# A depthwise convolution's last chunks on one core: order of gates, taps and sums

## The chip, the cores and the metric

The program runs on one core of one Trainium2 chip. The metric is device time in microseconds (us). The median of three runs of the kernel before is 1395.32 us (1394.76 to 1398.21).

## The reference

A two-layer decoder step is computed in float32 for 512 prompt tokens and 32 sample tokens (8 sequences of 4), 1024 features. The change lies in the convolution module of layer 0:

```python
a = h @ w_pw1 + b_pw1
u = a[..., :D_MODEL] * jax.nn.sigmoid(a[..., D_MODEL:])      # the GLU
ext = jnp.concatenate([hist.astype(u.dtype), u], axis=1)
v = lax.conv_general_dilated(ext, w_dw[:, None, :], (1,), 'VALID', ...) + b_dw   # 31 taps, each feature alone
v = layernorm(v, g_ln, b_ln)                                 # mean and variance over the 1024 features
y = jax.nn.silu(v) @ w_pw2 + b_pw2
```

A squared-ReLU MLP, a shared latent K/V, attention, a second MLP and a last norm follow. They are untouched.

## The kernel before, in words

Features lie on the 128 partitions, so the 1024 features are 8 chunks (`DC`), and the 544 tokens lie along the free dimension. Chunks are numbered 0 to 7 here. What is called the fifth chunk in the diff's neighbourhood is chunk 4, the seventh is chunk 6, and the last is chunk 7.

Each engine has its own queue, written out by hand in one block of the program, and runs it strictly in that order. The engines meet at semaphores. For chunk c of the convolution the work is:

- TensorE: two matrix products, number 2c (the gate half) and 2c+1 (the other half), each of 48 matmuls of 128x272 (`product`, L1623). Two chunks later come `tap_products(c)` (L1661): the 31 taps cut into groups of 4, each tap a matmul of 32 columns of weights against 512 tokens, on four copies of the input that are shifted by 0 to 3 tokens (`shifted`). `pe_steps(c)` says how many groups of 4 TensorE takes: 6 (24 taps) for chunks 0 to 6, all 8 for chunk 7. The result goes to PSUM bank 4 or 5 in turn (`conv_bank`), and bank 0 for chunk 7. From chunk 2 on the tap products wait on `conv_used` for the bank that chunk c-2 used.
- VectorE: `gates(c)` (L1094) scales the gate half, `gated(c)` (L1101 to L1104) makes the GLU output and writes it to `ext`. `sample_taps(c)` (L1112, L1115) does the 31 taps of the 32 sample tokens. `psum_taps(k)` (L1135, L1136) adds the taps that TensorE left out, 7 of them, of the chunk three before (`LATER` = 3). `statistics(k)` (L1163, L1144, L1152) centres the chunk by an early mean, which lies in banks 6 and 7, and adds the chunk and its square to the running sums `acc` and `acc2`. Chunk 6 is done otherwise: `dve_taps(6)` (L1122, L1124) does its seven left-out taps from `ext` in SBUF, ahead of TensorE's, and `finish(6)` (L1128) adds the two parts. Once chunk 6 is in the sums VectorE signals `stat_in`. When chunk 7's taps are there (`conv_mm`), L1203 makes `v` of chunk 7.
- ScalarE: the high halves of weights (`high`, L703; `ahead(u)` does those whose place the product u frees), the sigmoid (L759), the squares (`squares_after`, L717), and for chunk 7 half of the DMA issues that make the shifted copies (L766). The other half, and all of them for the other chunks, are issued by SyncE's queue (`shift`, L513), with the tap weights (L514).
- GpSimd: the low halves of weights (`low`, L575), each after its high half.

After chunk 7's taps TensorE turns the sums over the features into the layernorm's mean and variance: `small_part` (L1711, matmuls with a single moving column, 5 for each sum) of `acc` and `acc2` once `stat_in` has come, `mean_part` (L1706) of `acc` into banks 6 and 7, then the same of chunk 7's `v` and of its square. VectorE computes the variance from L1216 on, ScalarE takes the root, TensorE spreads it (L1728), and the second pointwise product starts (`product_pair`, L1674).

The order of the work around the change on VectorE is this loop:

```python
for c in range(DC):
    k = c - LATER
    if k >= 0:
        psum_taps(k)
        ...
        statistics(k)
    gates(c)
    gated(c)
    sample_taps(c)
    if c == DC - 2:
        dve_taps(c)
psum_taps(DC - LATER)
statistics(DC - LATER)
```

Of the kernel before, what the change touches and what calls it, by code (L numbers as in the profile page):

```python
# [24 lines left out]
DC = D // P  # L25
# [4 lines left out]
HALF = T // 2  # L30
# [6 lines left out]
TAPS = 31  # L37
# [3 lines left out]
GROUPS = P // SB  # L41
PE_TAPS = 24
STEPS = (TAPS + GROUPS - 1) // GROUPS
# [3 lines left out]
LATER = 3  # L47
# [26 lines left out]
VEC, at = {}, 0  # L74
# [7 lines left out]
CON, at = {}, 0  # L82
# [105 lines left out]
def decoder_program(nc, xT, hist, vecs, diags, cons, rope_tab, rows0, page_table, cache_ckv, cache_kpe, w_pw1, w_pw2, w_up, w_down,  # L188
# [17 lines left out]
    with ExitStack() as ctx:  # L206
# [3 lines left out]
        def sem(name):  # L210
# [12 lines left out]
        acc = sb("acc", [P, T])  # L223
# [10 lines left out]
        acc2 = sb("acc2", [P, T], F32, tap_mem)  # L234
# [3 lines left out]
        ps = ctx.enter_context(nc.psum_tensor("ps", [P, 8, 512], F32))  # L238
# [22 lines left out]
        invd = sb("invd", [P, P], F32, conv_mem)  # L261
# [68 lines left out]
        stat_in, mean_mm, small_mm, var_out, rs_out, rs_mm = (  # L330
            sem(n) for n in ("stat_in", "mean_mm", "small_mm", "var_out", "rs_out", "rs_mm"))
# [80 lines left out]

        def pe_steps(c):

            return PE_TAPS // GROUPS if c < DC - 1 else STEPS

        def moved(c, s, g):
            n = NP + GROUPS * (pe_steps(c) - 1)
# [259 lines left out]
        def _(act):  # L678
# [53 lines left out]
            def squares_after(c):  # L732
                for k in STAT_AFTER.get(c, ()):
                    sq_in()
                    square(v[:, k, :])
# [16 lines left out]
            for c in range(DC):  # L752
                if c == 0:
                    ahead(1)
                else:
                    squares_after(c - LATER)
                    ahead(2 * c)
                gate_()
                af.activation(t1[:, :], t1[:, :], ACT.Sigmoid, bias=V("b_pw1", DC + c)).then_inc(gate, 1)  # L759
                if c == DC - 1:  # L760
                    act.wait_ge(u_out, 2 * c + 1)
                    act.wait_ge(conv_mm, c - SLOTS + 1)
                    for s in range(GROUPS):
                        for g in range(GROUPS // 2, GROUPS):
                            to, of = moved(c, s, g)
                            act.dma_start(to, of).then_inc(shift_in[c % SLOTS], 16)  # L766
                if c > 0:
                    ahead(2 * c + 1)
            squares_after(DC - LATER)
# [261 lines left out]
        def _(dve):  # L1031
# [60 lines left out]
            def gates(c):  # L1092
                dve.wait_ge(mm, 2 * c + 1)
                df.tensor_tensor(halves(t1[:, :]), acc_of(2 * c), halves(rstd[:, :]), ALU.mult).then_inc(gate_in, 1)  # L1094
                dve.wait_ge(gate_in, c + 1)
                dve.sem_inc(freed, 1)
# [19 lines left out]

            def dve_taps(c):
                dst = v[:, c, 0:NP]
                for k in range(PE_TAPS, TAPS):
                    w, a = V("w_dw", c * TAPS + k), ext[:, c, k:k + NP]  # L1120
                    if k == PE_TAPS:
                        link(df.tensor_scalar(dst, a, w, None, ALU.mult))  # L1122
                    else:
                        link(df.scalar_tensor_tensor(dst, a, w, dst, ALU.mult, ALU.add))  # L1124
# [51 lines left out]

            for c in range(DC):
                k = c - LATER
                if k >= 0:
                    psum_taps(k)  # L1180
                    if k == EARLY:
                        early_mean()
                    statistics(k)
                gates(c)
                gated(c)
                sample_taps(c)
                if c == DC - 2:
                    dve_taps(c)
# [4 lines left out]
            k = DC - 2  # L1193
# [360 lines left out]
            for i in range(NSC):  # L1554
                dve.wait_ge(ks_mm, i + 1)
                m = st[:, i % SETS, 0:1]
# [39 lines left out]
        def _(pe):  # L1596
# [48 lines left out]
            def run(u0, n, ah, al, fresh=True):  # L1645

                for j in range(n):
                    product(u0 + j, ah, al, fresh and j == 0)
                    if j == 0:
                        sums()  # L1650

            def tap_products(c):
                pe.wait_ge(shift_in[c % SLOTS], 16 * (GROUPS * GROUPS + 1) * (c // SLOTS + 1))
                if 2 <= c < DC - 1:
                    pe.wait_ge(conv_used, c - 1)
                if c == DC - 1:
                    pe.wait_ge(freed, 2 * DC)
                n = pe_steps(c)
                for k in range(n):
                    for g in range(GROUPS):  # L1660
                        m = tf.matmul(ps[SB * g:SB * (g + 1), conv_bank(c), 0:NP], diag[:, c % SLOTS, GROUPS * k + g, :],  # L1661
                                      shifted[:, c % SLOTS, g, GROUPS * k:GROUPS * k + NP], start=(k == 0), stop=(k == n - 1))
                m.then_inc(conv_mm, 1)
# [37 lines left out]
            tap_products(DC - 2)  # L1701
            tap_products(DC - 1)

            def mean_part(a, begin, end):
                for h in range(2):
                    m = tf.matmul(ps[:, 6 + h, 0:HALF], invd[:, :], a[:, h * HALF:(h + 1) * HALF], start=begin, stop=end)  # L1706
                return m

            def small_part(bank, at, a):
                for j, b in enumerate(blocks5):  # L1710
                    m = tf.matmul(ps[:, bank, at + 2 * j:at + 2 * j + 1], a[:, b], invd[:, 0:1], start=True, stop=True)  # L1711
                return m

            pe.wait_ge(stat_in, 1)
            small_part(5, 0, acc)
            small_part(5, 1, acc2).then_inc(small_mm, 1)
            mean_part(acc, True, False)
            pe.wait_ge(sq_src, DC)
            small_part(4, 0, v[:, DC - 1, :])
            pe.wait_ge(sq_out, 2 * DC)  # L1720
# [382 lines left out]
```

## Time and profile before

| what | us |
|---|---|
| median of 3 runs | 1395.32 |
| lowest, highest | 1394.76, 1398.21 |
| profiled execution, its own time | 1399.37 |
| its span | 1397.6 |
| TensorE busy | 1358.2 (97%) |
| VectorE busy | 811.8 (58%) |
| ScalarE busy | 601.3 (43%) |
| GpSimd busy | 726.3 (52%) |

The profile is of one execution. PE is TensorE's matmuls, PEld its weight loads, DVE VectorE, ACT ScalarE, POOL GpSimd, SP SyncE; a q behind the name means the engine's queue issuing a DMA. Times are microseconds from the span's start. An end of a matmul is modelled, so its duration overlaps the next one's start, and in these rows a float32 matmul counts as two (x48 is 24 matmuls) where it isn't of the type fp32r. The mean granted TensorE clock is 0.984 of full speed.

### The profile page before, as it was taken

What the parts mean: (1) busy time and instruction counts of PE and PEld (TensorE: products, weight loads), DVE (VectorE), ACT (ScalarE), POOL (GpSimd) and SP (SyncE); (2) the same over time, 40 slices, a digit from 0 to 9 for tenths busy, and PEclk for the clock granted to TensorE, in tenths of its full rate; (3) what the DMA queues carried; (4) which work ended last, traced back from release to release, by engine and by line L of the source; (5) the groups of instructions that cost most, each with busy time, mean ns of one, the idle gap of its engine ahead of it and who ended that gap; (6) DMA issues with size and microseconds to landing.
All of it is one profiled execution on the core that took longest, in us unless ns stands there. A gap on an engine that the chain in (4) does not pass through costs nothing.

```text
span 1397.6 us, 26262 instructions
## 1 busy us (share of the span) xinstructions
PE 1358.2 (97%) x11038; PEld 1264.9 (91%) x11038; DVE 811.8 (58%) x1224; ACT 601.3 (43%) x1016; POOL 726.3 (52%) x505
## 2 busy tenths in 40 slices
PE   6999889999999999999999999999999999999997
PEld 6877489999999999999899867678999999999997
DVE  6689557655545463766555656554676364545534
ACT  5211255443434443434666544442364444443432
POOL 3322153587888785333323444330437888787741
PEclk9999789999999999999999999999999999999998
DMA  5755302222233324322111577670223222222221
GB/s 210 197 163 146 109 31 91 91 91 91 92 102 103 98 91 157 117 91 66 35 35 53 181 294 263 265 264 2 91 85 97 91 91 91 91 91 92 95 86 64
DMA packets 107204, 160.66 MB, mean 115 GB/s; under 512 B 7568, under 2 KB 91792, under 8 KB 101840
## 3 DMA queue, kind: packets, MB, share of 16 engines
q1 hardware_dynamic: 99536, 116.50, 26.3%
q0 software_dynamic: 7168, 41.95, 8.0%
q8 instruction: 87, 1.43, 0.4%
q10 hardware_dynamic: 384, 0.55, 0.1%
q14 instruction: 29, 0.24, 0.1%
HBM read 146.22 MB, written 4.03 MB: 108 GB/s over the span
## 4 chain that ended last, share of the span: by engine, by line
PE 92%; DVE 4%; ACT 1%; DMA 1%; issue 1%; ACTq 0%; POOL 0%; DVEq 0%; SPq 0%
PE ps L1623 33%; PE ps L1753 21%; PE ps L1741 18%; PE ps L1883 5%; PE ps L1923 3%; PE ps L1661 2%; PE ps L1972 2%; PE ps L1674 1%; PE ps L1953 1%; ACT wh L703 1%; PE ps L1963 1%; DMA x<-xT 0%; PE ps L1981 0%; PE ps L1711 0%; ACTq L766 0%
## 5 line engine op out<-in xcount | busy, mean ns | idle before, releaser
L575 POOL TENSOR_TENSOR wl<-raw,wh 128x512 fp32r<-128x512 f32 (+2 forms) x252 | 438.2, 1741 | 444.8 <-ACT wh L703 444.5
L703 ACT ACTIVATE wh<-raw 128x512 fp32r<-128x512 f32 (+2 forms) x253 | 192.7, 762 | 386.9 <-PE ps L1623 194.2
L1623 PE MATMUL ps<-xh,wh 128*128 128x272 f32 x704 | 148.6, 292 | 13.7 <-DVE xl L1049 11.1
L575 POOL TENSOR_TENSOR wl<-wuv,wh 128x512 fp32r<-128x512 f32 x104 | 135.2, 1311 | 48.1 <-ACT wh L703 48.0
L1753 PE MATMUL ps<-mh,wh 128*128 128x272 f32 x768 | 158.6, 288 | 0.0
L1753 PE MATMUL ps<-mh,wl 128*128 128x272 f32 x768 | 158.6, 288 | 0.0
L1753 PE MATMUL ps<-ml,wh 128*128 128x272 f32 x768 | 158.3, 288 | 0.0
L1623 PE MATMUL ps<-xh,wl 128*128 128x272 f32 x704 | 145.6, 289 | 0.0
L1623 PE MATMUL ps<-xl,wh 128*128 128x272 f32 x704 | 145.3, 288 | 0.0
L1623 PEld LDWEIGHTS ps<-xh,wh 128*128 128x128 f32 x704 | 110.9, 190 | 18.9 <-POOL wl L575 11.0
L1753 PEld LDWEIGHTS ps<-ml,wh 128*128 128x128 f32 x768 | 120.4, 188 | 0.0
L1753 PEld LDWEIGHTS ps<-mh,wh 128*128 128x128 f32 x768 | 120.3, 188 | 0.0
L1753 PEld LDWEIGHTS ps<-mh,wl 128*128 128x128 f32 x768 | 119.9, 189 | 0.0
L703 ACT ACTIVATE wh<-wuv 128x512 fp32r<-128x512 f32 x104 | 65.4, 630 | 113.7 <-DVE wuv L1292 74.8
L1623 PE MATMUL ps<-mh,wh 128*128 128x272 f32 x544 | 112.8, 288 | 1.4 <-POOL wl L575 1.4
L1623 PE MATMUL ps<-mh,wl 128*128 128x272 f32 x544 | 112.2, 288 | 0.0
L1623 PE MATMUL ps<-ml,wh 128*128 128x272 f32 x544 | 111.9, 287 | 0.0
L1623 PEld LDWEIGHTS ps<-xl,wh 128*128 128x128 f32 x704 | 110.9, 189 | 0.0
L1741 PE MATMUL ps<-th,wl 128*128 128x272 f32 x384 | 110.8, 289 | 0.0
L1741 PE MATMUL ps<-tl,wh 128*128 128x272 f32 x384 | 110.7, 288 | 0.0
L1741 PE MATMUL ps<-th,wh 128*128 128x272 f32 x384 | 110.5, 288 | 0.0
L1623 PEld LDWEIGHTS ps<-xh,wl 128*128 128x128 f32 x704 | 110.4, 190 | 0.0
(308 smaller groups left out, 3006.1 us busy)
## 6 DMA issues: line engine op xcount, KB each, us to landing
raw<-w_up SPq DMA_DIRECT2D x32, 1024.0 KB, 5.4
raw<-w_down SPq DMA_DIRECT2D x32, 1024.0 KB, 5.1
raw<-w_pw SPq DMA_DIRECT2D x11, 1024.0 KB, 6.0
shifted<-ext SPq DMA_DIRECT2D x112, 66.5 KB, 2.0
raw<-w_o SPq DMA_DIRECT2D x4, 1024.0 KB, 5.7
raw<-w_dq SPq DMA_DIRECT2D x3, 1024.0 KB, 5.3
raw<-w_uq SPq DMA_DIRECT2D x4, 768.0 KB, 4.4
diag<-diags SPq DMA_DIRECT2D x7, 384.0 KB, 3.8
```

The costliest lines, as they stand in the source:

```text
L575: pf.tensor_tensor(weight(wl, u), weight_raw(u), f32(weight(wh, u)), ALU.subtract).then_inc(w_lo, 1)
L703: af.activation(weight(wh, u), weight_raw(u), ACT.Copy).then_inc(w_hi, 1)
L1623: m = tf.matmul(ps[:, bank_of(u) + bank, 0:width], w[:, k, :], a[:, k, part], start=(k == 0 and n == 0), stop=(k == nk - 1 and n == 2))
L1661: m = tf.matmul(ps[SB * g:SB * (g + 1), conv_bank(c), 0:NP], diag[:, c % SLOTS, GROUPS * k + g, :], shifted[:, c % SLOTS, g, GROUPS * k:GR ...
L1674: m = tf.matmul(ps[:, 2 * (w_ % 2) + h, 0:HALF], weight(w, w_)[:, k, :], a[:, k, h * HALF:(h + 1) * HALF], start=(k == 0 and n == 0), stop ...
L1741: m = tf.matmul(factor_out(u, i), w[:, k, :], part(a, k), start=(k == 0 and n == 0), stop=(k == KH - 1 and n == 2))
L1753: m = tf.matmul(acc_of(u)[:, h, :], w[:, k, :], a[:, k0 + k, h * HALF:(h + 1) * HALF], start=(k0 == 0 and k == 0 and n == 0), stop=(k0 > 0 ...
L1883: m = tf.transpose(keys_at(n)[:, q * P:(q + 1) * P], a, ident)
L1923: m = tf.matmul(ps[NS * s:NS * (s + 1), 3 + i % 2, :], q, k, start=(c == 0), stop=(c == 2))
L1953: tf.matmul(out[:, c * NS:(c + 1) * NS], oc[:, (SPB * b + k) % SETS, cols], fold_w[:, b % 2, k, :], start=(k == 0), stop=False)
L1963: m = tf.transpose(ps[:, 5, q * P:(q + 1) * P], ss[:, q * P:(q + 1) * P], ident)
L1972: m = tf.matmul(ps[NS * s:NS * (s + 1), 6, 0:KL], pts[:, q, NS * s:NS * (s + 1)], latents(2 * i + s // 2)[:, r * KL:(r + 1) * KL], start=( ...
```

## The change

Four edits. On VectorE, the gate and the GLU of chunk 7 stand ahead of `psum_taps(4)` and `statistics(4)` instead of behind them. On ScalarE, the square of chunk 4 moves behind the sigmoid and the DMA issues of chunk 7 accordingly. `pe_steps` gives chunk 6 seven groups (28 taps) on TensorE, and `dve_taps(6)` does 3 taps instead of 7. The sums over chunks 0 to 6 (`acc`, `acc2`) are taken inside chunk 7's tap products, ahead of the last two groups, with the wait on `stat_in` that belongs to them; the two helpers are moved unchanged.

```diff
--- before.py
+++ after.py
@@ -412,7 +412,7 @@
 
         def pe_steps(c):
 
-            return PE_TAPS // GROUPS if c < DC - 1 else STEPS
+            return PE_TAPS // GROUPS + max(c - (DC - LATER), 0)
 
         def moved(c, s, g):
             n = NP + GROUPS * (pe_steps(c) - 1)
@@ -753,7 +753,8 @@
                 if c == 0:
                     ahead(1)
                 else:
-                    squares_after(c - LATER)
+                    if c < DC - 1:
+                        squares_after(c - LATER)
                     ahead(2 * c)
                 gate_()
                 af.activation(t1[:, :], t1[:, :], ACT.Sigmoid, bias=V("b_pw1", DC + c)).then_inc(gate, 1)
@@ -764,6 +765,7 @@
                         for g in range(GROUPS // 2, GROUPS):
                             to, of = moved(c, s, g)
                             act.dma_start(to, of).then_inc(shift_in[c % SLOTS], 16)
+                    squares_after(c - LATER)
                 if c > 0:
                     ahead(2 * c + 1)
             squares_after(DC - LATER)
@@ -1116,9 +1118,10 @@
 
             def dve_taps(c):
                 dst = v[:, c, 0:NP]
-                for k in range(PE_TAPS, TAPS):
+                first = GROUPS * pe_steps(c)
+                for k in range(first, TAPS):
                     w, a = V("w_dw", c * TAPS + k), ext[:, c, k:k + NP]
-                    if k == PE_TAPS:
+                    if k == first:
                         link(df.tensor_scalar(dst, a, w, None, ALU.mult))
                     else:
                         link(df.scalar_tensor_tensor(dst, a, w, dst, ALU.mult, ALU.add))
@@ -1176,13 +1179,17 @@
 
             for c in range(DC):
                 k = c - LATER
+                if c == DC - 1:
+                    gates(c)
+                    gated(c)
                 if k >= 0:
                     psum_taps(k)
                     if k == EARLY:
                         early_mean()
                     statistics(k)
-                gates(c)
-                gated(c)
+                if c < DC - 1:
+                    gates(c)
+                    gated(c)
                 sample_taps(c)
                 if c == DC - 2:
                     dve_taps(c)
@@ -1649,6 +1656,22 @@
                     if j == 0:
                         sums()
 
+            def mean_part(a, begin, end):
+                for h in range(2):
+                    m = tf.matmul(ps[:, 6 + h, 0:HALF], invd[:, :], a[:, h * HALF:(h + 1) * HALF], start=begin, stop=end)
+                return m
+
+            def small_part(bank, at, a):
+                for j, b in enumerate(blocks5):
+                    m = tf.matmul(ps[:, bank, at + 2 * j:at + 2 * j + 1], a[:, b], invd[:, 0:1], start=True, stop=True)
+                return m
+
+            def earlier_sums():
+                pe.wait_ge(stat_in, 1)
+                small_part(5, 0, acc)
+                small_part(5, 1, acc2).then_inc(small_mm, 1)
+                mean_part(acc, True, False)
+
             def tap_products(c):
                 pe.wait_ge(shift_in[c % SLOTS], 16 * (GROUPS * GROUPS + 1) * (c // SLOTS + 1))
                 if 2 <= c < DC - 1:
@@ -1657,6 +1680,8 @@
                     pe.wait_ge(freed, 2 * DC)
                 n = pe_steps(c)
                 for k in range(n):
+                    if c == DC - 1 and k == n - 2:
+                        earlier_sums()
                     for g in range(GROUPS):
                         m = tf.matmul(ps[SB * g:SB * (g + 1), conv_bank(c), 0:NP], diag[:, c % SLOTS, GROUPS * k + g, :],
                                       shifted[:, c % SLOTS, g, GROUPS * k:GROUPS * k + NP], start=(k == 0), stop=(k == n - 1))
@@ -1701,20 +1726,6 @@
             tap_products(DC - 2)
             tap_products(DC - 1)
 
-            def mean_part(a, begin, end):
-                for h in range(2):
-                    m = tf.matmul(ps[:, 6 + h, 0:HALF], invd[:, :], a[:, h * HALF:(h + 1) * HALF], start=begin, stop=end)
-                return m
-
-            def small_part(bank, at, a):
-                for j, b in enumerate(blocks5):
-                    m = tf.matmul(ps[:, bank, at + 2 * j:at + 2 * j + 1], a[:, b], invd[:, 0:1], start=True, stop=True)
-                return m
-
-            pe.wait_ge(stat_in, 1)
-            small_part(5, 0, acc)
-            small_part(5, 1, acc2).then_inc(small_mm, 1)
-            mean_part(acc, True, False)
             pe.wait_ge(sq_src, DC)
             small_part(4, 0, v[:, DC - 1, :])
             pe.wait_ge(sq_out, 2 * DC)
```

On VectorE, from the GLU of chunk 6 to the first taps of chunk 5, the program before has these rows (`t` is the gate's tile `t1`):

```order
L1122 TENSOR_SCALAR v<-ext,vec 128x512 [waits dve_at]
L1124 SCALAR_TENSOR_TENSOR v<-ext,vec,v 128x512 [waits dve_at] x6
L1135 SCALAR_TENSOR_TENSOR ps<-ext,vec,ps 128x512 [waits conv_mm,dve_at]
L1135 SCALAR_TENSOR_TENSOR ps<-ext,vec,ps 128x512 [waits dve_at] x5
L1136 SCALAR_TENSOR_TENSOR v<-ext,vec,ps 128x512 [waits dve_at]
L1163 SCALAR_TENSOR_TENSOR v<-v,vec,ps 128x544 [waits conv_used]
L1144 TENSOR_TENSOR acc<-acc,v 128x544 [waits sq_src]
L1152 TENSOR_TENSOR acc<-acc,sq 128x544 [waits sq_out,dve_at]
L1094 TENSOR_TENSOR t<-ps,rstd 128x544 [waits mm,sq_used]
L1101 TENSOR_TENSOR ps<-ps,rstd 128x2x272 [waits gate_in,mm]
```

And with the change:

```order
L1125 TENSOR_SCALAR v<-ext,vec 128x512 [waits dve_at]
L1127 SCALAR_TENSOR_TENSOR v<-ext,vec,v 128x512 [waits dve_at] x2
L1096 TENSOR_TENSOR t<-ps,rstd 128x544 [waits mm,dve_at]
L1103 TENSOR_TENSOR ps<-ps,rstd 128x2x272 [waits gate_in,mm]
L1105 SCALAR_TENSOR_TENSOR ext<-ps,vec,t 128x544 [waits gate,dve_at]
L1106 SCALAR_TENSOR_TENSOR exs<-ps,vec,t 128x8x4
L1138 SCALAR_TENSOR_TENSOR ps<-ext,vec,ps 128x512 [waits u_out,conv_mm]
L1138 SCALAR_TENSOR_TENSOR ps<-ext,vec,ps 128x512 [waits dve_at] x5
L1139 SCALAR_TENSOR_TENSOR v<-ext,vec,ps 128x512 [waits dve_at]
L1166 SCALAR_TENSOR_TENSOR v<-v,vec,ps 128x544 [waits conv_used]
L1147 TENSOR_TENSOR acc<-acc,v 128x544 [waits sq_src]
L1155 TENSOR_TENSOR acc<-acc,sq 128x544 [waits sq_out,dve_at]
```

The two waits on `mm` (the products 14 and 15) now stand ahead of chunk 4's taps and statistics, and four of the SBUF taps are gone.

On TensorE, the tap products of chunks 5 to 7 and the sums, before:

```order
L1661 MATMUL ps<-shifted,diag 32x512 [waits conv_used,shift_in2]
L1661 MATMUL ps<-shifted,diag 32x512 x23
L1661 MATMUL ps<-shifted,diag 32x512 [waits freed,shift_in3]
L1661 MATMUL ps<-shifted,diag 32x512 x31
L1711 MATMUL ps<-invd,acc 128x1 [waits stat_in]
L1711 MATMUL ps<-invd,acc 128x1 x9
L1706 MATMUL ps<-acc,invd 128x272 x2
L1711 MATMUL ps<-invd,v 128x1 [waits sq_src]
```

And with the change:

```order
L1686 MATMUL ps<-shifted,diag 32x512 [waits conv_used,shift_in2]
L1686 MATMUL ps<-shifted,diag 32x512 x27
L1686 MATMUL ps<-shifted,diag 32x512 [waits freed,shift_in3]
L1686 MATMUL ps<-shifted,diag 32x512 x23
L1666 MATMUL ps<-invd,acc 128x1 [waits stat_in]
L1666 MATMUL ps<-invd,acc 128x1 x9
L1661 MATMUL ps<-acc,invd 128x272 x2
L1686 MATMUL ps<-shifted,diag 32x512 x8
L1666 MATMUL ps<-invd,v 128x1 [waits sq_src]
```

The wait on `stat_in`, with the 12 matmuls behind it, has moved ahead of the last 8 tap matmuls, and chunk 6 has 4 tap matmuls more.

## Rows read from the trace of the kernel before

**Rows 1.** The page's chain that ended last, by engine, then one piece in order of time.
```profile
PE 92%; DVE 4%; ACT 1%; DMA 1%; issue 1%; ACTq 0%; POOL 0%; DVEq 0%; SPq 0%
...
149.48 3.82 DMA shifted<-ext
```

**Rows 2.** Timeline of PE: start, duration (us), line, operation, operands, count, [idle before].
```profile
126.35 0.52 PE L1623 MATMUL ps<-xh,wh 128*128 128x272 f32 x2
...
138.17 0.41 PE L1623 MATMUL ps<-xh,wl 128*128 128x272 f32 x2
138.51 10.51 PE L1661 MATMUL ps<-shifted,diag 128*32 128x512 f32 x96
153.34 9.88 PE L1661 MATMUL ps<-shifted,diag 128*32 128x512 f32 x64 [4.33 <-DMA shifted<-ext]
163.16 2.39 PE L1711 MATMUL ps<-invd,acc 128*128 128x1 f32 x20
165.41 1.72 PE L1706 MATMUL ps<-acc,invd 128*128 128x272 f32 x4
166.92 2.13 PE L1711 MATMUL ps<-invd,v 128*128 128x1 f32 x10
168.92 2.27 PE L1711 MATMUL ps<-invd,sq 128*128 128x1 f32 x10
171.05 2.16 PE L1706 MATMUL ps<-v,invd 128*128 128x272 f32 x4
173.00 2.18 PE L1728 MATMUL ps<-con,rs 128*128 128x128 f32 x10
```

**Rows 3.** Windows: busy PE, PEld, DVE, ACT, POOL, then granted clock, DMA share, GB/s.
```profile
151.00:153.30 2.30, 0.00 (x0) 0.00 (x0) 2.23 (x3) 1.25 (x3) 1.98 (x1) 0.77 0.53 196
...
157.00:159.00 2.00, 2.00 (x12) 0.39 (x8) 1.30 (x3) 0.30 (x1) 0.00 (x0) 0.50 1.05 344
159.00:161.00 2.00, 2.00 (x24) 0.57 (x20) 0.00 (x0) 0.00 (x0) 0.00 (x0) 0.99 0.93 391
...
165.40:167.00 1.60, 1.60 (x8) 1.23 (x7) 0.17 (x1) 0.00 (x0) 0.00 (x0) 0.65 0.00 0
```

**Rows 4.** Timeline of DVE, 123 to 172 us.
```profile
123.03 3.18 DVE L1112 TENSOR_TENSOR tap<-exs,vec 128x248 f32<-128x248 f32 x4
...
127.98 4.69 DVE L1124 SCALAR_TENSOR_TENSOR v<-ext,vec,v 128x512 f32<-128x512 f32 x6
...
138.24 0.78 DVE L1163 SCALAR_TENSOR_TENSOR v<-v,vec,ps 128x544 f32<-128x544 f32 x1
...
140.57 0.72 DVE L1094 TENSOR_TENSOR t<-ps,rstd 128x544 f32<-128x544 f32 x1
141.44 0.73 DVE L1101 TENSOR_TENSOR ps<-ps,rstd 128x544 f32<-128x544 f32 x1
...
143.30 1.40 DVE L1112 TENSOR_TENSOR tap<-exs,vec 128x248 f32<-128x248 f32 x4
...
145.96 4.71 DVE L1135 SCALAR_TENSOR_TENSOR ps<-ext,vec,ps 128x512 f32<-128x512 f32 x6
...
151.49 0.78 DVE L1163 SCALAR_TENSOR_TENSOR v<-v,vec,ps 128x544 f32<-128x544 f32 x1
...
157.41 0.73 DVE L1152 TENSOR_TENSOR acc<-acc,sq 128x544 f32<-128x544 f32 x1
...
163.38 0.75 DVE L1203 SCALAR_TENSOR_TENSOR v<-ps,vec,mean 128x512 f32<-128x512 f32 x1 [4.85 <-PE ps L1661]
```

**Rows 5.** The same timeline, further on: the variance's first step.
```profile
171.32 0.17 DVE L1216 TENSOR_TENSOR sm<-ps,sm 128x10 f32<-128x10 f32 x1 [5.57 <-PE ps L1711]
```

**Rows 6.** Timeline of ACT and its DMA issues, 143 to 157 us.
```profile
143.03 7.06 ACTq L766 DMA_DIRECT2D shifted<-ext  x8
...
152.30 0.66 ACT L717 ACTIVATE sq<-v 128x544 f32<-128x544 f32 x1 [1.05 <-DVE v L1163]
...
156.65 0.66 ACT L717 ACTIVATE sq<-v 128x544 f32<-128x544 f32 x1
```

**Rows 7.** Timeline of POOL.
```profile
120.20 4.75 POOL L575 TENSOR_TENSOR wl<-raw,wh 128x1024 fp32r<-128x1024 f32 x2 [12.89 <-ACT wh L703]
...
151.32 2.35 POOL L575 TENSOR_TENSOR wl<-raw,wh 128x1024 fp32r<-128x1024 f32 x1 [8.19 <-ACT wh L703]
```

## The prediction

> **What bounds the kernel now.** I read the chain of waits first: 92% of it is TensorE [rows 1], so work taken from the other engines counts only where TensorE stands still or runs slowly. Around the convolution's end the timeline of TensorE shows the places. The products 14 and 15 run from 126.35 to 138.58, about 6.1 us each. The tap products of chunks 5 and 6 follow until 149.0. Then TensorE idles 4.33 us for the shifted copies of chunk 7, and taps and sums follow until the variance can start at 171.32 [rows 2, 5]. The windows show that this idle time also halved the clock: 0.77 in the window at its end, 0.50 up to 159, 0.99 after [rows 3]. So chunk 7's 32 tap matmuls took 9.88 us, where 48 had taken 10.51 at full clock: 0.219 us each at 2.4 GHz, some 0.44 at 1.2.
>
> What to see on VectorE: from 123 to 158.14 it has hardly a gap [rows 4]. Its last step there (L1152, ends 158.14) sets `stat_in`, which TensorE needed only at 163.16, when chunk 7's taps were through. VectorE had 5.0 us to spare. The change spends this slack in two ways: it puts a wait into VectorE's queue, and it asks for `stat_in` 8 tap matmuls earlier.
>
> **The wait that moves on VectorE.** `gates(7)` needs product 14 and `gated(7)` product 15. Before, VectorE came to them at 140.57, after both were done. Now it comes after `dve_taps(6)`, which loses 4 taps of 0.79 us (4.69 us for six, with gaps) and ends at 129.5 instead of 132.7. Nothing the change does makes the products earlier. So VectorE idles until 132.6, runs L1094 for 0.72 us, and idles again until product 15 ends, 138.6. Queued behind it are chunk 4's taps and statistics, which before filled exactly this time (132.71 to 140.57). Idle time bought: 3.1 + 5.3 = 8.4 us; work saved: 3.1 us.
>
> Forward from 138.6, each step from a row of the same step [rows 4, 6]:
> - L1101 to L1104 take 1.8 us (as 141.44 to 143.2): `ext` of chunk 7 is written at 140.2, not 143.0, and VectorE is free at 140.4.
> - `psum_taps(4)` takes 5.55 us (145.96 to 151.49): ends 145.95.
> - `statistics(4)` takes 2.33 us (138.24 to 140.57). Its square now stands behind ScalarE's eight DMA issues, which take 7.06 us from 140.2 and so end at 147.3, where the square could have begun at 146.8. That is 0.6 us late: 148.9.
> - `sample_taps(7)` took 2.66 us (143.30 to 145.96), undisturbed. At chunk 6 its four L1112 took 3.18 us instead of 1.40 while GpSimd's weight pass ran to 124.95 [rows 7]. The last such pass moves: its high half stands behind the square on ScalarE, so it runs from 149.1 to 151.5 instead of from 151.32, now against L1112. It costs between nothing and its whole length of 2.35 us; I take 2.2, because the rows at chunk 6 show L1112 finishing about 1.25 us after the pass ends. Ends 153.8.
> - `psum_taps(5)`, 5.55 us: 159.3.
> - From L1163 of chunk 5 to `stat_in` 6.65 us (151.49 to 158.14). ScalarE sets most of it: its square of chunk 5, the state copies and a table load stand ahead of the square of chunk 6, 152.30 to 156.65. So the 1.2 us that a GpSimd pass cost there before isn't won back. `stat_in`: 166.0, against 158.1.
>
> On that GpSimd pass the Trainium skill (GPSIMD Engine Reference, Key points) says that GpSimd shares SBUF interfaces with VectorE, and that instructions with two SBUF inputs contend. The trace agrees by the 3.18 against 1.40 us. By the rule `psum_taps`, which has one input in PSUM, would not be slowed; were the pass to fall beside it instead of L1112, the sum would be 2.2 us lower.
>
> **TensorE up to the wait.** The tap products of chunk 5 run 138.5 to 143.8. Those of chunk 6 wait for `conv_used` of chunk 4, which moves from 138.2 to 145.95: a new idle time of 2.1 us. Then 28 matmuls x 0.219 = 6.1 us: 152.1. The shifted copies of chunk 7 landed 10.3 us after their input (143.0 to 153.3 [rows 1, 6]); now at 150.6, so they no longer stop anybody. 24 tap matmuls, 5.3 us: TensorE reaches the wait on `stat_in` at 157.4. Should the new idle time halve the clock, it costs what it cost before, 5.7 us at half speed, so 2.9 us: 160.3. Both are hidden, since `stat_in` comes at 166.0. The 4 added taps (0.9 us) and the slightly larger copies and tap weights of chunk 6 are hidden by the same cover; if it were gone they would cost 0.9 us. SyncE's queue issues as many DMAs as before; the weight load behind GpSimd's pass starts about 2 us sooner and has no reader until the second pointwise product.
>
> **TensorE after the wait.** It has stood for 5.7 to 8.6 us, longer than the 4.33 that halved the clock before, so I take 1.2 GHz. In the rows the one-column sums did not raise it: under them it fell (0.65 in the window from 165.4) and stayed low. From 166.0: the ten small sums of `acc` and `acc2` 4.1 us (as the two fives from 166.92 to 171.05), the mean part 1.95 (171.05 to 173.00), the 8 remaining taps 8 x 0.44 = 3.5: 175.55. Then the wait for L1203, 0.2 + 0.75, and the last ten small sums with the hand-over, 4.2 + 0.1: the variance starts at 180.8. Before: 171.32. **Sum: +9.5 us.** What follows is the same chain at the same low clock (root, L1728, first products), so it is passed on whole. At full clock the pieces after 166.0 would be 2.25, 0.75 to 1.5, 1.75, 0.95 and 2.4 (small sums as from 163.16 to 165.41, taps at 0.219): 174.1 to 174.9, or about +3.
>
> **The forecast.** The profiled execution took 1399.37 us, 1.8 above its span of 1397.6; its sum is 1408.9. It lies 4.05 above the median of the runs, 1395.32, outside their range. The added time is a chain of fixed steps, so I add it to the median: **1404.8 us**.
>
> **Rivals.**
> 1. The clock. If it comes back while the mean part and the last taps run, as it did under chunk 7's taps before, part of the taps and the last small sums go twice as fast: 0.75 + 1.9 us less, and some on the mean of chunk 7, so about +6, 1401.3. It took 5.7 us after 153.34 in the rows, and here mean part and taps together are 5.4 us long, so it is near. If it never falls, +3, 1398.3, which counts as no change. Against this second case speaks the idle time, longer than the one which halved it.
> 2. The other side, faster: the slack on VectorE decides. Were `stat_in` there when TensorE reaches it at 157.4, at full clock, sums (3.0 to 3.8 us) and 8 taps (1.75) end at 162.5, and 0.95 + 2.5 later the variance starts, at 166.0: -5.3, 1390.0. It is what earlier copies and an unbroken TensorE would buy. For it: the copies do come 2.8 us earlier and 4 VectorE taps go. It decides at `stat_in` before about 162.9 at full clock (171.3 - 8.4), and before 156.5 at half clock (171.3 - 14.8). Against it: VectorE's queue is in order, and product 15 doesn't end before 138.6; from there to `stat_in` are 27.4 us of rows.
> 3. The change does not do what it says: the tap products of chunk 6 could start late for another reason and TensorE reach the wait after `stat_in`. At half clock for all of the 52 taps it would arrive at 168.9, 2.9 us later: +12.4, 1407.7. Before, the clock came back under taps after 5.7 us, which speaks against it.
>
> **How the numbers follow.** About 0.3%, 4.2 us, is what can be told from no change. The likeliest case has 0.56, rival 1's partial recovery 0.17 and rival 3 0.04, all slower by over 0.3%: 0.77. Rival 1's full clock, and unseen gains of 3 to 5 us on VectorE (the GpSimd pass missing L1112, the square's place), make 0.15 within. Faster has 0.08. The range leaves out rival 2 at the lower end and nearly all of rival 3 above: low 1398.5 takes in full clock, high 1408.0 takes the sum plus the spread of the runs above their median, 2.9.
>
> **What would show it.** In the changed kernel's profile: gaps of VectorE ending at about 132.6 and 138.6, put down to TensorE; its GLU of chunk 7 at 139.4; the DMA issues from 140.2; a gap of TensorE from 143.8 to 146, ended by VectorE; no gap for the shifted copies; a gap inside chunk 7's taps up to about 166, ended by VectorE; clock 0.50 behind it; L1223 (before L1216) at about 180.8. Wrong in the sum if `stat_in` comes before 163; wrong in the price alone if the clock behind the wait is 1.0.

## The result, and the profile after

| | kernel before | changed |
|---|---|---|
| median of 6 runs each, us | 1395.76 | 1406.20 |
| lowest, highest | 1392.32, 1399.66 | 1404.97, 1408.27 |
| profiled execution, its span | 1397.6 | 1405.2 |
| ratio of the runs, 95% interval | | 1.0086 (1.0065 to 1.0107) |

The change makes the kernel slower by 12 us by the ratio (9 to 15), 10.4 by the medians. The prediction was 1404.8 in a range of 1398.5 to 1408.0, slower with a chance of 0.77. One run of the kernel before on the last chip used below (2240.63 us at a mean granted clock of 0.556) is left out of the comparison there.

The two profiled executions differ by a constant before the place of the change: the changed kernel runs 1.40 us ahead from its first loads on. So I compare distances from one fixed point, the start of chunk 5's tap products, which follow product 15 at once. It is at 138.51 before [rows 2] and at 137.11 after. Timeline of TensorE in the changed kernel (start, duration, line, operation, operands, count, idle time before and what ended it):

```profile
137.11 5.36 PE L1686 MATMUL ps<-shifted,diag 128*32 128x512 f32 x48
145.07 11.37 PE L1686 MATMUL ps<-shifted,diag 128*32 128x512 f32 x104 [2.61 <-DVE v L1139]
164.31 4.43 PE L1666 MATMUL ps<-invd,acc 128*128 128x1 f32 x20 [7.87 <-DVEq L1207]
168.60 2.16 PE L1661 MATMUL ps<-acc,invd 128*128 128x272 f32 x4
170.69 3.47 PE L1686 MATMUL ps<-shifted,diag 128*32 128x512 f32 x16
175.11 1.28 PE L1666 MATMUL ps<-invd,v 128*128 128x1 f32 x10 [0.95 <-DVE v L1210]
176.25 1.36 PE L1666 MATMUL ps<-invd,sq 128*128 128x1 f32 x10
```

The wait for the shifted copies of [rows 2] is gone. Two new ones stand there, both ended by VectorE: 2.61 us ahead of chunk 6's taps (for `conv_used`), and 7.87 us inside chunk 7's taps (for `stat_in`). The reason is in VectorE's timeline:

```profile
126.58 1.54 DVE L1127 SCALAR_TENSOR_TENSOR v<-ext,vec,v 128x512 f32<-128x512 f32 x2
131.31 0.72 DVE L1096 TENSOR_TENSOR t<-ps,rstd 128x544 f32<-128x544 f32 x1 [3.20 <-PE ps L1630]
137.22 0.73 DVE L1103 TENSOR_TENSOR ps<-ps,rstd 128x544 f32<-128x544 f32 x1 [5.18 <-PE ps L1630]
...
139.43 4.71 DVE L1138 SCALAR_TENSOR_TENSOR ps<-ext,vec,ps 128x512 f32<-128x512 f32 x6 [0.50 <-DVE exs L1106]
...
147.30 3.59 DVE L1114 TENSOR_TENSOR tap<-exs,vec 128x248 f32<-128x248 f32 x4
...
157.68 0.78 DVE L1166 SCALAR_TENSOR_TENSOR v<-v,vec,ps 128x544 f32<-128x544 f32 x1
...
163.47 0.72 DVE L1155 TENSOR_TENSOR acc<-acc,sq 128x544 f32<-128x544 f32 x1 [1.19 <-ACT sq L717]
...
177.74 0.17 DVE L1223 TENSOR_TENSOR sm<-ps,sm 128x10 f32<-128x10 f32 x1 [2.61 <-PE ps L1666]
```

In [rows 4] VectorE worked through from 123 to 158. Now it stands 3.20 us for product 14 and 5.18 us for product 15, with chunk 4's taps behind it (L1138, from 139.43). `stat_in` comes with the end of L1155, at 164.2: 27.1 us after the fixed point instead of 19.6. The variance starts at 177.74, 40.6 us after it, against 32.8 before [rows 5]. The clock, by windows (columns as in [rows 3]):

```profile
158.00:160.00 2.00, 0.00 (x0) 0.00 (x0) 1.91 (x3) 1.50 (x2) 0.00 (x0) 1.00 0.00 0
160.00:162.00 2.00, 0.00 (x0) 0.00 (x0) 1.91 (x3) 1.98 (x3) 0.00 (x0) 0.55 0.00 0
...
172.00:174.00 2.00, 2.00 (x12) 0.20 (x4) 0.00 (x0) 0.00 (x0) 0.00 (x0) 0.54 0.00 0
174.00:176.00 2.00, 1.04 (x12) 0.89 (x9) 0.82 (x2) 0.66 (x1) 0.00 (x0) 1.00 0.00 0
```

It held through the gap of 2.61 us and through all 52 taps after it, fell some 4 us into the long wait, and came back at about 173.9, as the last of the eight taps ran. ScalarE and GpSimd beside it:

```profile
138.80 5.47 ACTq L767 DMA_DIRECT2D shifted<-ext  x8
145.78 0.66 ACT L717 ACTIVATE sq<-v 128x544 f32<-128x544 f32 x1 [12.78 <-DVE v L1166]
```
```profile
147.46 2.50 POOL L575 TENSOR_TENSOR wl<-raw,wh 128x1024 fp32r<-128x1024 f32 x1 [12.63 <-ACT wh L703]
```

The last GpSimd pass starts 0.16 us after the sample taps, and these take 3.59 us instead of 1.40. In the kernel before it fell on a step of the statistics, which took 1.96 us where the same step otherwise takes 0.72 (VectorE's timeline before):

```profile
152.30 1.96 DVE L1144 TENSOR_TENSOR acc<-acc,v 128x544 f32<-128x544 f32 x1
```

From the variance on everything is the old chain, later: the same VectorE instructions are 8.3 us later at 218 us and 9.2 us later from 810 us on, counted from the fixed point. The chain of waits over the whole span reads nearly as in [rows 1], with ScalarE at 2% for 1% and DMA at 0% for 1%:

```profile
PE 92%; DVE 4%; ACT 2%; issue 1%; POOL 0%; DMA 0%; DVEq 0%; SPq 0%; ACTq 0%
```

Its share says nothing of the 12 us; only the timeline of this stretch does.

### The profile page after: what moved, and what is told of

Its sections match the earlier page's. It is cut to its first block, busy times and chain, and to the rows that moved or that the text cites. A ratio compares the mean times of both kernels' runs of the same rounds, so it can differ in the third digit from the quotient of the medians.

```text
span 1405.2 us, 26273 instructions
## 1 busy us (share of the span) xinstructions
PE 1358.8 (97%) x11046; PEld 1265.5 (90%) x11046; DVE 807.8 (57%) x1220; ACT 600.6 (43%) x1016; POOL 726.4 (52%) x505
## 4 chain that ended last, share of the span: by engine, by line
PE 92%; DVE 4%; ACT 2%; issue 1%; POOL 0%; DMA 0%; DVEq 0%; SPq 0%; ACTq 0%
PE ps L1630 33%; PE ps L1764 21%; PE ps L1752 18%; PE ps L1894 5%; PE ps L1934 3%; PE ps L1686 2%; PE ps L1983 2%; PE ps L1699 1%; DVE ps L1138 1%; PE ps L1964 1%; ACT wh L703 1%; PE ps L1974 0%; PE ps L1666 0%; PE ps L1992 0%; PE ps L1841 0%
## 5 line engine op out<-in xcount | busy, mean ns | idle before, releaser
L1630 PE MATMUL ps<-xh,wh 128*128 128x272 f32 x704 | 148.4, 292 | 12.7 <-DVE xl L1051 10.1
```

What stands on the lines that cost most here:

```text
L1630: m = tf.matmul(ps[:, bank_of(u) + bank, 0:width], w[:, k, :], a[:, k, part], start=(k == 0 and n == 0), stop=(k == nk - 1 and n == 2))
```

## The experiments

The theory: the first edit alone makes the loss, because VectorE's queue is in order, and what it holds back (chunk 4's taps and statistics) sets `stat_in`. The rivals: the sums inside the taps are what costs; the earlier copies pay after all; the half clock plays no part. Four kernels with parts of the change ran beside the same runs of the kernel before, on another chip.

**The order alone.** From the kernel before:

```diff
             for c in range(DC):
                 k = c - LATER
+                if c == DC - 1:
+                    gates(c)
+                    gated(c)
                 if k >= 0:
                     psum_taps(k)
...
-                gates(c)
-                gated(c)
+                if c < DC - 1:
+                    gates(c)
+                    gated(c)
```

with the square of chunk 4 behind the DMA issues on ScalarE, as in the change. These two can't be parted: the square waits for chunk 4's statistics, which VectorE now makes only after the GLU, and the GLU waits for the sigmoid, which stood behind the square.

> Chunk 7's gate and GLU ahead of chunk 4's taps (with the square behind the DMA issues), nothing else of the change. Measure: from the end of product 15 to the variance's first step, 32.7 us before, 40.5 with the whole change. Theory (VectorE's queue is held until product 15 ends and so stat_in is late): VectorE idles 5 us and more before the GLU, stat_in comes some 27 us after product 15 as with the whole change, TensorE waits for it behind all 32 tap matmuls, and the variance is 3 to 6 us later than before; total +3 to +6 us. Rival (the sums inside the taps are the cost, the order is harmless): within 1 us of before. Rival (earlier copies pay): 2 us or more faster.

Ratio 1.0072 (1.0043 to 1.0100), variance 37.5 us after the fixed point. TensorE's timeline:

```profile
137.77 5.36 PE L1667 MATMUL ps<-shifted,diag 128*32 128x512 f32 x48
145.38 12.22 PE L1667 MATMUL ps<-shifted,diag 128*32 128x512 f32 x112 [2.25 <-DVE v L1138]
164.63 4.42 PE L1717 MATMUL ps<-invd,acc 128*128 128x1 f32 x20 [7.03 <-DVEq L1206]
```

It brings both new waits and a loss of 4.7 us in the trace, where the theory had 3 to 6. The runs lose more, 10.1 us (6.0 to 14.0), above the forecast of the total; the same excess comes back in most of the experiments and is taken up below. The earlier copies win nothing here.

**28 taps alone.**

```diff
-            return PE_TAPS // GROUPS if c < DC - 1 else STEPS
+            return PE_TAPS // GROUPS + max(c - (DC - LATER), 0)
...
-                for k in range(PE_TAPS, TAPS):
+                first = GROUPS * pe_steps(c)
+                for k in range(first, TAPS):
```

> 28 taps of chunk 6 on TensorE and 3 on VectorE, nothing else of the change. Theory: VectorE comes to chunk 7's gate 3.1 us sooner (137.4 in the time of the profile before), so just ahead of product 15's end, and its GLU is as early as with the order changed, while chunk 4's taps are already done. stat_in about 17 us after product 15, copies landed 12 us after it, TensorE without a gap of over 1 us, at full clock: variance 25 to 27 us after product 15 against 32.7, total 5.5 to 8 us faster than before. Rival (taps moved to TensorE cost what they take, TensorE is the bound): 1 us slower to no change. Rival (the clock falls all the same): 3 us faster.

Ratio 0.9991 (0.9971 to 1.0012). The trace is as the theory said (the variance 0.8 us sooner than its 25 to 27), timelines of VectorE and of TensorE:

```profile
138.02 0.72 DVE L1094 TENSOR_TENSOR t<-ps,rstd 128x544 f32<-128x544 f32 x1
139.19 0.73 DVE L1101 TENSOR_TENSOR ps<-ps,rstd 128x544 f32<-128x544 f32 x1 [0.44 <-PE ps L1624]
...
155.93 0.73 DVE L1153 TENSOR_TENSOR acc<-acc,sq 128x544 f32<-128x544 f32 x1 [1.22 <-ACT sq L717]
...
163.26 0.17 DVE L1217 TENSOR_TENSOR sm<-ps,sm 128x10 f32<-128x10 f32 x1 [3.42 <-PE ps L1712]
```
```profile
139.08 18.23 PE L1662 MATMUL ps<-shifted,diag 128*32 128x512 f32 x168
157.24 2.39 PE L1712 MATMUL ps<-invd,acc 128*128 128x1 f32 x20
```

VectorE comes to the GLU 0.44 us before product 15 ends, with chunk 4's taps done, and TensorE runs all 84 tap matmuls without a gap. The variance starts after 24.2 us instead of 32.8: 8.6 us sooner. But the runs gained 1.3 us only (4.1 faster to 1.7 slower), against a forecast of 5.5 to 8. That stayed open here.

**The sums inside alone.** `earlier_sums` ahead of the last two groups of chunk 7's taps, the rest as before:

```diff
                 for k in range(n):
+                    if c == DC - 1 and k == n - 2:
+                        earlier_sums()
                     for g in range(GROUPS):
```

> Sums of seven chunks ahead of the last 8 tap matmuls of chunk 7, nothing else of the change. Theory: stat_in (as before, 19.5 us after product 15) is there before TensorE comes to it, so nothing waits; sums that ran beside VectorE's step for chunk 7 now stand ahead of it, but run at the full clock, and it comes out within 1.5 us of before. Rival (the sums inside are what costs): 3 us or more slower. Rival (they are what gains, and the order spoils it): 2 us or more faster.

Ratio 1.0020 (1.0002 to 1.0038); variance after 32.1 us, 0.7 sooner than before in the trace. TensorE doesn't wait for `stat_in`. The trace says what the theory said; the runs are 2.8 us slower (0.3 to 5.3), outside the 1.5 us of the theory and 3.5 above the trace, which stayed open here too.

**28 taps and the sums inside**, the change less its first edit and the place of the square that goes with it (the diff is from the kernel before):

```diff
-            return PE_TAPS // GROUPS if c < DC - 1 else STEPS
+            return PE_TAPS // GROUPS + max(c - (DC - LATER), 0)
...
                 for k in range(n):
+                    if c == DC - 1 and k == n - 2:
+                        earlier_sums()
                     for g in range(GROUPS):
```

> 28 taps of chunk 6 and the sums inside, without the order of gate and GLU: the change less its first edit. Theory (the first edit alone makes the loss): faster than before by 5 to 8 us, faster than the whole change by 14 to 18; stat_in is there when TensorE comes to it, about 17 us after product 15. Rival (the loss comes from the sums inside, by a wait): no faster than before.

Ratio 0.9996 (0.9972 to 1.0020), so the change without its first edit isn't shown slower than before. The forecast of 5 to 8 us faster was missed; "no faster than before" was what the rival expected, a loss from the sums inside by a wait. In the trace it wins less than the 28 taps alone: the variance comes after 29.7 us, not 24.2. The runs of the two can't be told apart (3.9 faster to 2.8 slower, 4.1 faster to 1.7 slower). TensorE's timeline:

```profile
137.60 16.70 PE L1680 MATMUL ps<-shifted,diag 128*32 128x512 f32 x152
155.27 3.06 PE L1660 MATMUL ps<-invd,acc 128*128 128x1 f32 x20 [0.97 <-DVEq L1201]
158.18 2.16 PE L1655 MATMUL ps<-acc,invd 128*128 128x272 f32 x4
160.27 3.57 PE L1680 MATMUL ps<-shifted,diag 128*32 128x512 f32 x16
164.79 1.27 PE L1660 MATMUL ps<-invd,v 128*128 128x1 f32 x10 [0.95 <-DVE v L1204]
```

Here the third edit shows its own price. TensorE waits 0.97 us for `stat_in`, and under the one-column sums the clock falls (0.70 from 156 to 158). The mean part takes 2.16 us and the eight taps 3.57, as at 1.2 GHz, where the 28 taps alone had 1.16 us for the mean part and ran all their taps, which stand ahead of the sums, at full clock. So the rival is right in this much: the sums inside cost 5.5 us of the trace here. They don't make the loss of the change, which the order alone brings without them.

Then four more, with the kernel before as one of them, on a third chip.

**The kernel before against itself**, and **the 28 taps again**:

> The kernel before, unchanged, against itself. Two questions: what the comparison shows when nothing differs (theory: within 2 us, ratio interval holding 1.000; rival: the kernel of a run comes out 3 to 5 us slower than the kernel before whatever it is, which would explain why the 28 taps alone gained 1 us where its trace gained 8.6), and how long the stretch of the sample attention with its gathers is in a trace of the same chip (theory: some 9 us longer than in the first chip's trace, as in the traces of the four experiments, so that it is the chip's).

> The 28 taps alone, a second time, beside the kernel before against itself. Theory: the variance again 24 to 26 us after product 15 and the stretch up to the attention 8 us shorter than before; if the total is again only 1 us shorter than before, the gain is given back later, and the trace of the kernel before on the same chip shows in which stretch. Rival (chance): total 6 to 9 us shorter.

The kernel before against itself: 0.9999 (0.9982 to 1.0015). Its trace has the wait for chunk 7's input too, ended this time by the tap weights, and a clock that falls after it:

```profile
152.05 8.77 PE L1661 MATMUL ps<-shifted,diag 128*32 128x512 f32 x64 [3.46 <-DMA diag<-diags]
```

The 28 taps: 0.9973 (0.9952 to 0.9994), 3.8 us faster (0.8 to 6.7), with the variance after 25.4 us in the trace. The attention stretch was on this chip as long as in the first trace, against what was expected of it, both in the kernel before and with the 28 taps (in both the VectorE instructions keep their distance to the first trace's within 0.1 us from 820 to 1000 us). In the four traces of the first experiments, on the other chip, it was 5.9 to 9.1 us longer, 7.4 for the same 28 taps. So that stretch is no trait of a kernel, and the gain is not given back there.

What separates the trace from the runs is, as far as the record shows, the clock. Each run's record has its mean granted clock. The 28 runs of the kernel before in this comparison have 0.984 to 0.992, median 0.9895, and their times go with it (correlation -0.94: the longer runs are those with the lower mean clock). Both traces of the kernel before are of executions with 0.984, the lowest of that range. A mean lower by 0.0055 is 2 x 0.0055 x 1397 = 15 us more at 1.2 GHz. Some of it lies in this stretch, by windows of the kernel before (its first trace) and of the 28 taps on this chip:

```profile
140.00:200.00 60.00, 51.11 (x351) 35.77 (x343) 35.32 (x53) 25.37 (x34) 20.57 (x12) 0.80 0.24 72
```
```profile
140.00:200.00 60.00, 54.99 (x418) 42.75 (x407) 35.34 (x50) 28.45 (x38) 22.15 (x13) 0.91 0.26 80
```

That is 24 us at 1.2 GHz against 11; the second trace of the kernel before has 0.83, so 20. The traces of the 28 taps (0.989 and 0.991) and of the change (0.985) lie at or near the medians of their runs (0.988, 0.990; 0.985). (The second trace of the change, below, is the other way round: 0.989, where its runs have 0.9855.) So the kernel before is in its typical run faster than its traces: their executions took 1399.37 us against a median of 1395.32, and 1399.90 against 1393.61, so 4 to 6 us more. Every gain read against them was too large and every loss too small, by about 4 us. The 4 us is the difference between the 28 taps' 7.4 us (their second trace against the first of the kernel before, from the fixed point to 218 us) and the runs' 3.8. It is worked out from totals; no plain run shows in which place its clock fell.

**The change less its third edit** (order and 28 taps, sums behind all taps), from the changed kernel:

```diff
-                    if c == DC - 1 and k == n - 2:
-                        earlier_sums()
...
             tap_products(DC - 1)
+            pe.wait_ge(stat_in, 1)
+            small_part(5, 0, acc)
+            small_part(5, 1, acc2).then_inc(small_mm, 1)
+            mean_part(acc, True, False)
```

> The change less its third edit: order and 28 taps, but the sums behind all taps. Theory: stat_in comes 27 us after product 15 as with the whole change; the 8 tap matmuls and VectorE's step for chunk 7 no longer stand behind it, so the variance comes 36.5 to 38 us after product 15, against 40.6 with the whole change and 32.7 before: 4 to 5 us slower than before. Rival (the 8 taps behind the wait cost nothing): 40 us and more.

Ratio 1.0063 (1.0040 to 1.0086), variance after 37.8 us, in the forecast range. The runs are 8.8 us slower (5.6 to 12.0), above the 4 to 5 forecast. The third edit costs 2.8 us of the trace within the whole change (40.6), 1.6 against that kernel's second trace (39.4). One row differs from the whole change in its clock:

```profile
147.85 14.78 PE L1668 MATMUL ps<-shifted,diag 128*32 128x512 f32 x120 [2.61 <-DVE v L1139]
```

These 60 taps would take 13.1 us at 0.219 each. Behind the same gap of 2.61 us the clock fell here (0.59 from 148 to 150, 0.56 from 150 to 152). It costs nothing, since TensorE waits for `stat_in` all the same.

**The change with TensorE kept busy in its wait:**

```diff
             def earlier_sums():
+                for _ in range(8):
+                    tf.matmul(ps[:, 3, 0:NP], invd[:, :], x[:, 0, 0:NP], start=True, stop=True)
                 pe.wait_ge(stat_in, 1)
```

> The whole change, and eight float32 matmuls of 128x512 without use (into a PSUM bank that nobody reads then) ahead of the wait on stat_in, some 6.9 us at full clock, so that TensorE is busy for most of its 7.9 us wait. Theory (of the loss the part behind stat_in is the half clock): the clock is at 2.4 GHz when stat_in comes and through the sums of acc and acc2 or most of them; variance 35 to 38 us after product 15 against 40.6, so 3 to 5 us faster than the change, still 2 to 5 slower than before. Rival (the clock plays no part, the order of waits does all): 40.6 us again, or more by what the added matmuls delay.

Ratio 1.0057 (1.0037 to 1.0078), variance after 36.6 us, 4.0 less than the first trace of the change. The runs are 7.9 us slower than the kernel before (5.2 to 10.9), above the 2 to 5 forecast. TensorE's timeline has every piece from the added matmuls to the variance at full clock; ahead of them the clock fell once more behind the gap of 2.61 us (0.50 from 150 to 152), so that the 52 taps took 13.06 us for 11.37:

```profile
139.40 5.36 PE L1688 MATMUL ps<-shifted,diag 128*32 128x512 f32 x48
147.37 13.06 PE L1688 MATMUL ps<-shifted,diag 128*32 128x512 f32 x104 [2.61 <-DVE v L1139]
160.36 7.13 PE L1671 MATMUL ps<-x,invd 128*128 128x512 f32 x16
167.33 2.29 PE L1666 MATMUL ps<-invd,acc 128*128 128x1 f32 x20
169.48 1.16 PE L1661 MATMUL ps<-acc,invd 128*128 128x272 f32 x4
170.57 1.92 PE L1688 MATMUL ps<-shifted,diag 128*32 128x512 f32 x16
```

`stat_in` is as late as in the change (27.1 us after the fixed point; the added matmuls end 0.9 us after it), so about half of the trace's 7.8 us is the clock, and the rest the lateness alone. By the second trace of the change (39.4) the clock's part is 2.8 us; the runs, 7.9 us slower against 12 and 11.5, have the same sign but overlapping intervals.

**The kernel before with TensorE kept busy** (four such matmuls between chunk 6's and chunk 7's taps), and **the change again**, on a fourth chip:

```diff
             tap_products(DC - 2)
+            pe.wait_ge(freed, 2 * DC)
+            for _ in range(4):
+                tf.matmul(ps[:, 3, 0:NP], invd[:, :], x[:, 0, 0:NP], start=True, stop=True)
             tap_products(DC - 1)
```

> The kernel before with four float32 matmuls of 128x512 without use (3.4 us at full clock) in TensorE's wait for chunk 7's shifted copies. So far each changed kernel came out some 4 us longer against the kernel before in the timed runs than its trace says up to the attention (28 taps alone: trace -7.4, runs -3.8; the whole change: trace +8.3, runs +12), while the kernel before against itself showed nothing. Theory: in plain runs the kernel before has a shorter wait for its copies than under the profiler and keeps the clock, so its own traces are 4 us too slow; then this kernel gains in its trace (variance 28 to 30 us after product 15 against 31.3 and 32.7) but 1 us at most in the runs. Rival: the clock falls in plain runs as in the trace; then it is 2 to 4 us faster in the runs as well, and the 4 us stay open.

> The whole change again, beside the same runs of the kernel before. Theory: variance 40 to 41 us after product 15, stat_in 27 us after it, and 8 to 12 us slower than the kernel before; the clock behind the wait 0.50 until at least the mean part.

The first: 1.0003 (0.9991 to 1.0016), though its trace has the variance after 27.0 us, 5.8 sooner than the trace of the kernel before:

```profile
147.75 3.70 PE L1704 MATMUL ps<-x,invd 128*128 128x512 f32 x8
151.45 7.07 PE L1661 MATMUL ps<-shifted,diag 128*32 128x512 f32 x64
```

Taps at full clock (7.07 us against 9.88) gain nothing in the runs. The likeliest reading is that in most plain runs of the kernel before the clock isn't lost at this wait, or is lost for less; there is no trace of the kernel before from this chip that would show it. The other comparison confirms the change: 1.0082 (1.0066 to 1.0097), 11.5 us slower, variance after 39.4 us in the trace (forecast 40 to 41), with the clock back during the last eight taps:

```profile
164.78 4.43 PE L1666 MATMUL ps<-invd,acc 128*128 128x1 f32 x20 [7.87 <-DVEq L1207]
169.07 2.16 PE L1661 MATMUL ps<-acc,invd 128*128 128x272 f32 x4
171.16 2.36 PE L1686 MATMUL ps<-shifted,diag 128*32 128x512 f32 x16
```

All of them side by side; the second column is from the fixed point to the variance in the trace.

| kernel | variance after, us | ratio of runs (95%) |
|---|---|---|
| before, two traces | 32.8, 31.4 | 0.9999 (0.9982 to 1.0015) |
| whole change, two traces | 40.6, 39.4 | 1.0086 (1.0065 to 1.0107), 1.0082 (1.0066 to 1.0097) |
| order alone | 37.5 | 1.0072 (1.0043 to 1.0100) |
| order and 28 taps | 37.8 | 1.0063 (1.0040 to 1.0086) |
| change, TensorE kept busy | 36.6 | 1.0057 (1.0037 to 1.0078) |
| sums inside alone | 32.1 | 1.0020 (1.0002 to 1.0038) |
| 28 taps and sums inside | 29.7 | 0.9996 (0.9972 to 1.0020) |
| before, TensorE kept busy | 27.0 | 1.0003 (0.9991 to 1.0016) |
| 28 taps alone, two traces | 24.2, 25.4 | 0.9991 (0.9971 to 1.0012), 0.9973 (0.9952 to 0.9994) |

The offset can be checked over the whole table. Taken as they are, the shifts of the traces against 32.8 lie inside the interval of the runs for one of the ten comparisons with a changed kernel (28 taps and sums inside). With 4 us added to each they do for eight; the first trace of the 28 taps (-4.6 us, where the interval ends at -4.1) and the kernel before kept busy (-1.8, interval from -1.3) stay outside. So one offset of the kernel before accounts for most of the excess.

## Why the prediction was right, point by point

- **The wait that moves on VectorE**: right, and it is the cause. Idle time forecast 3.1 and 5.3 us, measured 3.20 and 5.18. The order alone, without the other edits, shows it.
- **`stat_in` at 166.0**: measured 164.2, which is 165.6 with the 1.40 us put back. Of the steps, the GpSimd pass cost 2.2 us on the sample taps as taken (3.59 against 1.40), so it did fall on these and not on `psum_taps`. The 0.6 us for a late square was not spent: ScalarE's eight DMA issues took 5.47 us, not 7.06, and the square began when its input came.
- **TensorE up to the wait**: right within 0.5 us (gap 2.61 for 2.1, arrival 156.4 + 1.4 = 157.8 for 157.4); the clock held in both traces of the change. In two other kernels it fell behind the same gap and was hidden, as the prediction had it for that case. Rival 3 didn't happen. Its 1407.7 lay inside the range, though the prediction says that the range leaves nearly all of it out.
- **TensorE after the wait**: the ten sums 4.3 us for 4.1, the mean part 2.1 for 1.95, the taps 3.5 for 3.5. The last ten small sums were mis-sized: the clock came back at about 173.9 and they took 2.5 us, not 4.1. So the variance is 7.8 us later in the trace, not 9.5: rival 1's partial recovery, somewhat later than it had it.
- **Adding the sum to the median**: this step failed, and hid the last one. I noted that the profiled execution lay 4 us above the median and outside the runs, and took that for a constant. It was an execution with a lower mean clock than most runs of the same kernel. Measured from typical runs the change costs about 4 us more than the trace says: 7.8 + 4 is the 12 us of the ratio (the medians say 10.4). That the total came out inside the range was luck in this much: the two errors, 1.7 and about 4 us, have opposite signs. With the last sums sized right the same sum gives 1403.1, and with both set right about 1407.
- **Rival 2** (faster): its deciding point was right. With `stat_in` early (the 28 taps alone, 17.6 us after the fixed point) the copies' early arrival does pay (8.6 and 7.4 us in the traces, 1.3 and 3.8 in the runs, of which only the second is clear of noise); the change's own first edit removes that condition.
- The 4 added taps on TensorE cost nothing visible behind the late `stat_in` (37.8 us with them, 37.5 without), as said, and the edit that contains them is the only one that gains.

What stays open: in how many plain runs of the kernel before the clock falls at the copies' wait, and whether the profiler makes it likelier. The runs give a mean clock each, not its place.

## What to carry to other kernels

Moving a step that waits ahead of work that doesn't, on an in-order engine, costs the whole wait unless the engine arrives after the event anyway; shorten what stands before the step instead, as the 28 taps do, and it comes early without holding anything. Before a trace is used as the baseline of a sum, compare its mean clock with that of the plain runs: here 0.984 against 0.9895 was about 4 us, as much as the 28 taps gain. Parts of a change can cancel each other: by the runs one gained 1 to 4 us (28 taps), one lost about 10 (order) and one about 3 (sums inside).

## What the runs showed of the hardware

- One-column float32 matmuls, though TensorE counts as busy throughout, did not keep the clock up: it fell under them or right after in [rows 3], with the 28 taps alone (0.57 in the window from 162 to 164, with no gap of TensorE since chunk 5's taps) and in the kernel with the 28 taps and the sums inside, where it took the eight tap matmuls behind them with it (3.57 us for 1.92); there a gap of 0.97 us stood ahead of them as well. In the change with TensorE kept busy it held through the same sums.
- The length of an idle gap did not settle the clock: behind the same gap of 2.61 us it held in both traces of the change and fell in two other kernels (0.59 from 148 to 150 with order and 28 taps, 0.50 from 150 to 152 with TensorE kept busy). It fell at the waits of 3.46, 4.18 (sums inside alone) and 4.33 us in all three traces that have them, though, as argued from the runs, not as a rule, and inside the wait of 7.87 us in both.
- A GpSimd pass over SBUF held VectorE's instructions with two inputs in SBUF: four multiplications took 3.59 us beside a pass of 2.50 that began 0.16 us after them, 1.40 alone, and an addition to `acc` 1.96 for 0.72.
- The stretch of the sample attention, which gathers by DMA, differed between traces of the same program on two chips by 7.4 us (820 to 1000 us, the 28 taps). The medians of the kernel before on the three chips of the experiments are 1404.0, 1393.6 and 1399.7 us.
